# Eight experts run as one flat sequence of steps, with the gather, the selection and the scatter placed inside the steps

## The reference

```
logits = ht @ router                       # 256 tokens, 8 experts
top_val, top_idx = lax.top_k(logits, 2)
gates = softmax(top_val)
combine = sum(one_hot(top_idx, 8) * gates[..., None], axis=1)
for e in range(8):
    out += combine[:, e:e+1] * swiglu(ht, w1[e], w3[e], w2[e])
# swiglu(h, w1, w3, w2) = (silu(h @ w1) * (h @ w3)) @ w2, with 3584 hidden columns
```

## Time and profile before

| | |
|---|---|
| median of three runs | 2586.34 us (2583.64 to 2587.12) |
| span of the profiled execution | 2586.1 us |
| TensorE busy | 2179.1 us, 84% |
| VectorE busy | 1696.9 us, 66% |
| ScalarE busy | 1369.9 us, 53% |
| expert stage | from about 845 to 1926 us |

### The profile page before, as it was taken

One profiled execution on the slowest core, in us unless ns is written; L12 is line 12 of the kernel. 1 busy time (PEld: TensorE's weight loads), 2 busy tenths in 40 slices (PEclk: granted clock), 3 DMA queues, 4 the chain that ended last, 5 costly groups with the idle time before them and its releaser, 6 DMA issues.

```text
span 2586.1 us, 29301 instructions
## 1 busy us (share of the span) xinstructions
PE 2179.1 (84%) x9596; PEld 1761.5 (68%) x9596; DVE 1696.9 (66%) x2035; ACT 1369.9 (53%) x1848; POOL 46.3 (2%) x80
## 2 busy tenths in 40 slices
PE   3854779987647899999999999999978997766997
PEld 3733668866436687878787878787857885655886
DVE  5377377753453797979797979797976554324554
ACT  2422234433321687878787878787863444333443
POOL 1010000000000000000000000000000000000000
PEclk9955689988556899999999999999999998867999
DMA  9433358733003597979797979797964553202451
GB/s 369 163 146 114 107 200 318 306 134 128 1 17 137 229 374 289 372 284 375 286 374 284 375 281 379 278 378 287 372 251 157 184 181 128 81 1 98 179 195 49
DMA packets 80544, 572.69 MB, mean 221 GB/s; under 512 B 9088, under 2 KB 9728, under 8 KB 12272
## 3 DMA queue, kind: packets, MB, share of 16 engines
q1 hardware_dynamic: 70112, 508.59, 51.8%
q0 software_dynamic: 7936, 57.05, 5.9%
q10 hardware_dynamic: 2448, 6.41, 0.7%
HBM read 570.97 MB, written 1.05 MB: 221 GB/s over the span
## 4 chain that ended last, share of the span: by engine, by line
PE 71%; issue 12%; DVE 9%; ACT 6%; DMA 1%; POOL 1%; ACTq 0%; POOLq 0%; DVEq 0%
PE ps L528 20%; PE ps L530 20%; PE ps L529 20%; PE ps L738 2%; PE ps L714 2%; ACT arena L1089 1%; PE ps L807 1%; PE ps L816 1%; PE ps L637 1%; ACT arena L1141 1%; DMA arena<-in_ada 1%; PE ps L791 1%; DVE ps L1452 1%; DVE xt_low L1359 1%; ACT arena L1096 1%
## 5 line engine op out<-in xcount | busy, mean ns | idle before, releaser
L1625 DVE TENSOR_TENSOR weights_low<-ring,weights_high 128x1024 fp32r<-128x1024 f32 x672 | 801.6, 1222 | 68.3 <-ACT weights_high L1125 43.6
L528 PE MATMUL ps<-weights_high,xt_high 128*128 128x512 f32 x1808 | 737.7, 408 | 63.3 <-DVE weights_low L1625 42.3
L1125 ACT ACTIVATE weights_high<-ring 128x1024 fp32r<-128x1024 f32 x672 | 708.2, 1058 | 78.6 <-PE ps L530 70.0
L530 PE MATMUL ps<-weights_high,xt_low 128*128 128x512 f32 x1808 | 719.0, 398 | 0.0
L529 PE MATMUL ps<-weights_low,xt_high 128*128 128x512 f32 x1808 | 718.5, 397 | 0.0
L1366 DVE TENSOR_TENSOR weights_low<-ring,weights_high 128x1024 fp32r<-128x1024 f32 x294 | 357.7, 1224 | 249.0 <-ACT weights_high L960 247.5
L960 ACT ACTIVATE weights_high<-ring 128x1024 fp32r<-128x1024 f32 x294 | 307.2, 1057 | 373.9 <-PE ps L530 359.0
L528 PEld LDWEIGHTS ps<-weights_high,xt_high 128*128 128x128 f32 x1808 | 349.1, 193 | 145.9 <-DVE weights_low L1625 47.3
L530 PEld LDWEIGHTS ps<-weights_high,xt_low 128*128 128x128 f32 x1808 | 347.7, 192 | 75.2
L529 PEld LDWEIGHTS ps<-weights_low,xt_high 128*128 128x128 f32 x1808 | 350.0, 194 | 71.0 <-issue 1.9
L528 PE MATMUL ps<-weights_high,hT_high 128*128 128x512 f32 x712 | 279.2, 392 | 4.2 <-DVE hT_low L1403 4.2
(11 more groups left out here) (194 smaller groups left out, 1536.2 us busy)
## 6 DMA issues: line engine op xcount, KB each, us to landing
ring<-in_stream SPq DMA_DIRECT2D x483, 1024.0 KB, 4.9
Z<-in_ada POOLq DMA_DIRECT2D x42, 1024.0 KB, 5.1
arena<-in_ada POOLq DMA_DIRECT2D x6, 1024.0 KB, 16.2
Z<-in_na POOLq DMA_DIRECT2D x1, 2048.0 KB, 9.7
Z<-in_dil POOLq DMA_DIRECT2D x1, 2048.0 KB, 15.9
band<-in_band ACTq DMA_DIRECT2D x2, 768.0 KB, 18.9
X<-in_x SPq DMA_DIRECT2D x1, 1024.0 KB, 5.1
gate_mix<-in_rows ACTq DMA_DIRECT2D x2, 512.0 KB, 9.6
```

The source lines that it names most:

```text
L528: nc.tensor.matmul(out, xh, wh, start=n, stop=False, skip_group_check=True)
L530: return nc.tensor.matmul(out, xl, wh, start=False, stop=last, skip_group_check=True)
L1125: act.activation(WH[:, slot, :], raw, ACT.Copy).then_inc(m["hi_ready"], 1)
L1625: nc.vector.tensor_tensor(WL[:, slot, :], raw, WH[:, slot, :].bitcast(F32), ALU.subtract).then_inc(m["lo_ready"], 1)
```

## The change

The eight experts are laid end to end as 112 steps. Host code orders the weight stream accordingly (`expert_chunks`), so that the last downs of one expert lie among the pieces of the next expert's first steps. The loop is now over pairs of experts, three times by `Fori` and once written out without its end; 20 steps are unrolled in it, and an inner loop of three times two steps stands in each expert. The gathered tokens alternate between two homes. The selection is transposed after step 3 of an expert, and VectorE builds the next selection right behind; the gather for the next expert stands after step 6, ScalarE's first four copies of it before step 7, the other four and the high part before step 13, the low part after step 13. The result is copied in step 1 of the next expert; the first half is scattered there ahead of the downs and the second half behind them. The combining weight is applied when the scattered rows are added, not in the selection. Clearing by matmul is gone: the first down product of an expert starts the sum afresh. A small SiLU stands ahead of the whole stage.

```diff
+        XGH = [XTH[:, a:a + 4, :].rearrange("p a (c s) -> p (a c) s", c=2) for a in (0, 4)]
+        XGL = [XTL[:, a:a + 4, :].rearrange("p a (c s) -> p (a c) s", c=2) for a in (0, 4)]
 # TensorE
+                def step(c, pair, t):
+                    k = pair * (2 * EX_STEPS) + t * 2 + c
+                    e = pair * 2 + c // EX_STEPS
+                    if c % EX_STEPS == 0:
+                        pe.wait_ge(m["xg_ready"], e + 1)
+                    ups(3 * c - 1, c, t, pieces, range(1))
+                    pe.wait_ge(m["h_ready"], k)
+                    turn_h(1 - c % 2)
+                    ups(3 * c - 1, c, t, pieces, range(1, 4))
+                    scatters = c % EX_STEPS == 1 and c > 1
+                    if scatters:
+                        pe.wait_ge(m["ye_ready"], e)
+                        scatter(0, 2)
+                    pe.wait_ge(m["hT_ready"], k)
+                    downs(3 * c + 1, c - 1, t, pieces)
+                    if scatters:
+                        pe.wait_ge(m["sc_added"], e * 2)
+                        scatter(1, 2)
+                def expert_events(c, pair):
+                    if c % EX_STEPS == 3:
+                        turn_selection(e + 1)
+                    if c % EX_STEPS == 6:
+                        pe.wait_ge(m["sc_added"], e * 2 + 1)
+                        gather(e + 2)
+                def two_experts(pair, last):
+                    for sub in range(2):
+                        c0 = EX_STEPS * sub
+                        end = last and sub == 1
+                        for c in range(c0 + 3, c0 + 7):
+                            step(c, pair, 0)
+                            if not (end and c == c0 + 6):
+                                expert_events(c, pair)
+                        with pe.Fori(0, 3) as t:
+                            for c in (c0 + 7, c0 + 8):
+                                step(c, pair, t)
+                        for c in range(c0 + 13, c0 + 17 - 3 * end):
+                            step(c, pair, 0)
-                with pe.Fori(0, EXPERTS) as e:
-                    ups(0, 0, 0, e_pieces, range(4))
-                    scatter(e + 1)
...
-                    clear_y(range(2))
...
-                    gather(e + 2)
-                    pe.wait_ge(m["hT_ready"], k_e + EX_STEPS)
-                    downs(EX_CHUNKS - 1, 1, 0, e_pieces, True)
 # ScalarE
+                    for i in (1, 2, 3):
+                        if i == 3 and c % EX_STEPS == 1 and c > 1:
+                            act.wait_ge(m["piece_done"], t * (2 * RING) + pieces + (m["freed"] + 2 * up))
                             copy_ye()
...
+                            step(c, pair, 0)
+                            expert_events(c, pair)
+                        if not end:
+                            gathered(pair * 2 + sub + 2, range(4))
+                        with act.Fori(0, 3) as t:
+                            for c in (c0 + 7, c0 + 8):
+                                step(c, pair, t)
+                        if not end:
+                            gathered(pair * 2 + sub + 2, range(4, KT))
+                        for c in range(c0 + 13, c0 + 17 - 3 * end):
+                            if c == c0 + 13 and not end:
+                                gathered_hi(pair * 2 + sub + 2, 1 - sub)
+                            step(c, pair, 0)
+                act.activation(sgt[:, 0, 0:1], cols[:, 0:1], ACT.Silu).then_inc(m["ct_ready"], 1)
 # VectorE
+                def select_next(e):
+                    dve.wait_ge(m["ct_ps"], e + 1)
+                    take_rank(bass.ds(e + 1, 1))
+                    nc.vector.tensor_copy(r_cb, ...).then_inc(m["sel_copied"], 1)
+                    dve.wait_ge(m["sel_copied"], e + 2)
+                    select()
+                def add_scattered(number, b, bank):
+                    dve.wait_ge(m["sc_ps"], number)
+                    nc.vector.scalar_tensor_tensor(YB[:, b, :], ps[:, bank:bank + 2, :]..., r_cb[:, b:b + 1], YB[:, b, :],
+                                                   ALU.mult, ALU.add).then_inc(m["sc_added"], 1)
+                    for i in range(4):
+                        if i == 1 and c % EX_STEPS == 2 and c > 2:
+                            add_scattered(e * 2, 1, 2)
+                        lo(up + i // 2, i % 2, t, pieces)
+                        if i == 0:
+                            h_product(1 - c % 2, k)
+                    hT_low(1 - c % 2, k)
+                    if c % EX_STEPS == 1 and c > 1:
+                        add_scattered(e * 2 - 1, 0, 2)
+                    for half in range(2):
+                        lo(up + 2, half, t, pieces)
...
+                            if c == c0 + 3:
+                                select_next(e)
...
+                            if c == c0 + 13 and not end:
+                                gathered_lo(e + 2, 1 - sub)
 # host
+def expert_chunks(w1, w3, w2):
+    def wide(w):
+        return w.transpose(1, 0, 2).reshape(w.shape[1], -1)
+    return ffn_chunks(wide(w1), wide(w3), w2.reshape(-1, D))
```

More of the change, by code:

```diff
@@ L792, in turn_h, with downs @@
                     mm.then_inc(m["hT_ps"], 1)
-                def downs(local, par, turn, e_pieces, last):
+                def downs(local, n, turn, e_pieces):
+                    par = n % 2
                     for f in range(2):
@@ L809, in gather, with scatter @@
                     mm.then_inc(m["xg_ps"], 1)
[L811 to L818, removed]
-                clear_y(range(2))
+                def scatter(b, bank):
+                    for half in range(2):
+                        mm = nc.tensor.matmul(ps[:, bank + half, :], CT[:, b, :], YE[:, half * 512:(half + 1) * 512],
+                                              start=True, stop=True)
+                    mm.then_inc(m["sc_ps"], 1)
@@ L860, in experts @@
-                scatter(EXPERTS + 1)
-                pe.wait_ge(m["sc_added"], 2 * EXPERTS + 2)
+                pe.wait_ge(m["xg_ready"], 1)
+                ups(0, 0, 0, 0, range(4))
+                step(1, 0, 0)
+                step(2, 0, 0)
+                with pe.Fori(0, EXPERTS // 2 - 1) as pair:
+                    two_experts(pair, False)
+                two_experts(EXPERTS // 2 - 1, True)
+                n = EXPERTS * EX_STEPS - 1
+                pe.wait_ge(m["h_ready"], n + 1)
@@ L863, in _ @@
+                turn_h(n % 2)
+                pe.wait_ge(m["hT_ready"], n + 1)
+                downs(EX_TOTAL - 1, n, 0, 0)
+                pe.wait_ge(m["ye_ready"], EXPERTS)
+                scatter(0, 2)
+                scatter(1, 0)
+                pe.wait_ge(m["sc_added"], 2 * EXPERTS + 1)
             pe.wait_ge(zero_ready, 1)
@@ L1144, in gathered, with gathered_hi @@
+                def gathered_hi(number, held):
                     act.wait_ge(m["xg_full"], number)
-                    act.activation(XGH, XG, ACT.Copy).then_inc(m["xg_hi"], 1)
+                    act.activation(XGH[held], XG, ACT.Copy).then_inc(m["xg_hi"], 1)
                 def copy_ye():
                     act.activation(YE, ps[:, 0:2, :].rearrange("p j n -> p (j n)"), ACT.Copy).then_inc(m["ye_ready"], 1)
[L1150 to L1158, removed]
-                            copy_ye()
[L1160 to L1165, removed]
-                    for half in range(2):
[L1167 to L1185, removed]
@@ new lines, in expert_events, with two_experts @@
+                def expert_events(c, pair):
+                    e = pair * 2 + c // EX_STEPS
+                    j = c % EX_STEPS
+                    if j == 4:
+                        copy_selection(e + 1)
+                def two_experts(pair, last):
+                    for sub in range(2):
+                        c0 = EX_STEPS * sub
+                        end = last and sub == 1
+                        for c in range(c0 + 3, c0 + 7):
+                            step(c, pair, 0)
[11 more added lines that the diff above has]
+                            step(c, pair, 0)
@@ new lines, in experts @@
+                act.activation(sgt[:, 0, 0:1], cols[:, 0:1], ACT.Silu).then_inc(m["ct_ready"], 1)
+                gathered(1, range(KT))
+                gathered_hi(1, 0)
+                for i in range(4):
+                    hi(i // 2, i % 2, 0, 0, 0)
+                step(1, 0, 0)
+                step(2, 0, 0)
+                with act.Fori(0, EXPERTS // 2 - 1) as pair:
+                    two_experts(pair, False)
+                two_experts(EXPERTS // 2 - 1, True)
+                n = EXPERTS * EX_STEPS - 1
@@ L1186, in experts @@
+                silu(2 * (3 * n) + 2, n % 2, 0, 0)
+                for half in range(2):
+                    hi(EX_TOTAL - 1, half, 0, 0, 0)
+                hT_high(n % 2, n + 1)
                 act.wait_ge(m["piece_done"], m["freed"] + 2 * EX_TOTAL)
@@ new lines, in add_scattered, with step @@
+                def add_scattered(number, b, bank):
+                    dve.wait_ge(m["sc_ps"], number)
```

(41 more changed lines are left out.)

139 lines of the change are left out of this document (44 added, 95 removed).

## The result

The changed kernel takes 2640.0 us (median of four runs, 2636.7 to 2643.7) against 2585.0 (four runs) before: ratio 1.0212, 95% interval 1.0199 to 1.0226, so 55 us slower. The forecast was slower, 2610 us, with a range of 2588 to 2625; the direction held, the size did not. The profiled execution has a span of 2639.4 us against 2586.1.

The account below looks back on a forecast made before the run. The prediction took TensorE to set the pace, VectorE close behind. Seven boundaries at +3.85 us (+26.9), the ends and +6.1 of clock summed to +23.9 us on 2586.1: 2610, range 2588 to 2625.

Parts of the forecast that it names:

- rival 3: At the outer loop's jumps back, 20 unrolled steps are too long to be held: +4 to +12 us, 2618; chance 0.14.
- the lump ahead of step 13: ScalarE's second half of the copies and the high part, 1.4 + 1.05 us, leave TensorE 0.5 us of wait.
- the step of the scatters: Two scatters per expert: 3.43 us of TensorE work, with stalls of 2.6 us in step 1 and 1.0 in step 2.
- the step of the selection: After step 3 TensorE transposes the selection, 0.22 us, then stands 2.1 us while VectorE builds the next.
- the sum: All terms together: 26.9 - 1.25 + 1.75 - 9.65 + 6.1 = +23.9 us, giving 2610; chance 0.58.
- Stalls in each expert: TensorE's waits: gather 4.05, copies before step 13 0.5, first scatter 2.6, second 1.0, selection 2.1; together 10.3 us.
- the 1.5 us of cover: In the inner loop a split piece is ready 1.5 us before TensorE wants it; shorter delays were taken as hidden.
- Clock at the other stalls: The 2.6 us stall at the first scatter may lose 0 or 1.75 us of clock seven times; half taken, +6.1.
- The gather's step: After step 6: 3.46 us of gather, then TensorE stands 4.05 us for four copies and the first new piece.
- The ends: Start: -1.25 us for the table load, +1.75 for the first clock ramp; last expert: -9.65 us.
- Rival 1: The stalls after the gathers and at the scatters do not lower the clock: +5.5 us, 2592; chance 0.17.
- Rival 2: Four split slots hide the gather; its 4.05 us stall and clock loss vanish seven times: -40.6 us, 2569; chance 0.11.

Follow-up runs that it names:

- e4: The changed kernel with the outer loop over pairs of experts written out, so it never jumps back: 2631.9 us, ratio 1.0186.
- e1: The changed kernel with VectorE building the next selection after step 4 instead of after step 3: 2617.8 us, ratio 1.0138.
- e2: The changed kernel with TensorE gathering after step 5 instead of after step 6: 2607.7 us, ratio 1.0085.
- e3: The changed kernel with VectorE's two additions of scattered rows moved behind the pieces TensorE needs next: 2603.6 us, ratio 1.0072.
- e8: e6 with the high part of the gathered tokens made after step 13 instead of before it: 2521.4 us, ratio 0.9752.
- e6: e5 with the outer loop over pairs of experts written out: 2532.0 us, ratio 0.9788.
- e9: e8 without the second sweep, the code for experts with more than 128 tokens, which is not run here but jumped past: 2523.5 us, ratio 0.9766.
- e7: The kernel before the change with only a small SiLU added ahead of the experts: 2577.8 us, ratio 0.9961.
- e5: The changed kernel with the moves of e1, e2 and e3 together, the outer loop still a loop: 2540.5 us, ratio 0.9816.

## Why the prediction was right in direction and wrong in size

The mechanism of the sum, stalls in fixed places of each expert and the clock behind them, is what the trace shows. The step that failed most is the two jumps back, which the sum put at nothing and left to rival 3: they cost 8.1 us of kernel time (e4) and 10.2 in the trace of the changed kernel. Four smaller terms were too low as well: the lump ahead of step 13, the clock, the step of the scatters and the step of the selection.

**Stalls in each expert.** Right, in place and size: 4.05, 0.5, 2.6, 1.0 and 2.1 us against 3.80, 0.40, 2.51, 0.90 and 2.17. Taking away the four long ones gave back their length at least; e1, e2 and e3 show that they, and not the stream or VectorE's load, hold TensorE. That they hold it at all follows from the places where an engine's written order puts a wait for TensorE ahead of the piece that TensorE needs next.

**"Of which the 1.5 us of cover and ScalarE's own lead leave 0.5 us of wait."** The wait was 0.4 us, but the price was not the wait. The transposes of h mark the steps:

```profile
970.57 0.38 PE L791 MATMUL ps<-unit,FS 128*128 128x128 f32 x2
...
979.68 0.38 PE L791 MATMUL ps<-unit,FS 128*128 128x128 f32 x2
```

That step lasted 9.11 us, the next 8.61 and the third 8.43, 0.9 us in all over 8.41. The step that failed is that a lump costs only where it first stops TensorE; seven times 0.4 us were missing. Moving half of the lump gave 7.0 us in the stage (e8), 1.0 for each of seven experts.

**"Clock at the other stalls: ... I take half."** Mis-sized and misplaced. The granted clock fell behind the gather seven times, behind the selection five times and behind the first addition once: 13 losses in the trace, against 10.5 in the sum, at some 1.7 us each. The stall of 2.17 us lost it in most experts and the one of 2.51 mostly did not, while in e2 the same 2.51 lost it six times of seven; so length alone does not decide it. Taking half for the longer of the two and nothing for the shorter had one row of 2.22 us behind it; that the count came within 2.5 is in part luck.

**Rival 3, loops too long to be held.** It was given 0.14 and +4 to +12 us on top of the sum, and it is what happened. In the trace the two jumps make their pairs of steps 5.4 and 4.8 us longer than elsewhere; e4 and e6 show 8.1 and 8.5 us. The forecast left it out of the sum because no row of before showed such a pause; its loop bodies were shorter. The Trainium skill, "Runtime: NRT & Kernel Launch", Instruction fetch mechanics, has a taken branch to a target that is not held wait for that code to be fetched; the packets of the instruction queues inside the pause agree, and so does the pause at a jump forward (e9). The runs show the jump as the cause; that the time is the fetch itself is not shown. It rests on when those packets come, and straight code brings nearly as many over a run without a pause.

**Not thought of.** The jump past the second sweep, whose code had grown too: 2.5 us against 0.3 before. The first scatter and its step and the next: with both waits 7.4 us over two plain steps, where the sum had 3.43 + 2.6 + 1.0 = 7.0. And the attention stage of the second block, which no edit touches, took 4 us more: the same 264 instructions of TensorE, at a granted clock of 0.57 instead of 0.65, in the stretches that answer each other, before and after:

```profile
2245.00:2334.00 89.00, 56.48 (x264) 47.46 (x264) 28.36 (x46) 29.42 (x76) 1.01 (x1) 0.65 0.03 12
```

```profile
2294.00:2387.00 93.00, 61.15 (x264) 51.81 (x264) 27.86 (x46) 29.82 (x76) 1.01 (x1) 0.57 0.03 12
```

**The account.** Missing between 2610.0 and 2639.4: jumps back 10.2, lumps 0.4 x 7 = 2.8, scatters 0.4 x 7 = 2.8, the step with the selection 0.3 us longer than summed, eight times, 2.4, clock 13 x 1.7 - 18.4 = 3.7, jump forward 2.2, attention 3.8. The gather's step came out as summed. That is 27.9 of 29.4; the other 1.5 are not assigned. All these are readings of one execution; those of the clock and of attention can differ in another.

**The ends and rivals 1 and 2.** The gain of the table load is confirmed on its own (e7: 9.7 us for eight loads of 1.28, and the start's wait 1.24 us shorter, against 1.25 summed). Rival 1 fell: with a 3.8 us stall the clock was lost at all seven gathers. Rival 2 fell, as the wait of 3.80 us shows: no split pieces lay ready behind ScalarE's copies.

## What to carry to other kernels

Where engines run in written order, place a wait for another engine behind the work that this engine needs next, and as late as its own consumer allows: five small moves and a written-out outer loop turned +2% into -2.5% for the same merge of loops. Test such moves together too: while one stall is left, the clock can fall there, and the single gains come out too small. Divide lumps on the feeding engines so that each part is smaller than the lead, since a used-up lead goes on costing for steps. A loop body of 20 unrolled steps paid 4 to 5 us at each jump back; written out it paid nothing.

## What the runs showed of the hardware

A jump back over the long body stopped ScalarE (3.5 and then 3.9 us, as it came to its next stretch of code; 2.9 us in e5) and TensorE (2.0 to 2.5 us) where no work held them; VectorE's waits there name ScalarE. A jump forward past the second sweep stopped VectorE for 2.5 us. The short bodies of before and of the inner loops showed no such pause, nor did the same steps written out. The length of a wait alone did not decide whether the clock fell: it fell behind a wait of 2.51 us in one of seven experts (changed kernel) and in six of seven (e2), behind 3.70 us at six of seven boundaries (e7), behind 3.80 us at all seven gathers (changed kernel). The Trainium skill, "ScalarE: Activation LUTs", What ACT_TABLE_LOAD costs, adds a drain of some 1380 ns to a switch of tables; taking eight switches off the path gave 1.24 us apiece in the stall, so on this path only the load counted and no drain shows. And the same code behind the stage took 654.3 or 662.5 us in the executions of e8 and e9, with the clock at half level for 128 or 161 us of it: a few microseconds at the far end of a kernel should not be put down to an edit in front of it.
